# Sliding-window attention scores of the prompt tiles as two fp32r products of stacked high and low halves

## The reference, cut to what matters

```python
def swa_prompt(q, k, v, sinks_hg):          # CHUNK = 64, WINDOW = 128
    ...
    s = jnp.einsum('bcqhgd,bckhd->bchgqk', qc, kb) * SWA_SCALE
    key_chunk = jnp.arange(nc)[:, None] - WINDOW_CHUNKS + (jnp.arange(nk) // CHUNK)[None, :]
    s = jnp.where((key_chunk >= 0)[None, :, None, None, None, :], s, -jnp.inf)
    p = sink_softmax(s, sinks_hg)
    o = jnp.einsum('bchgqk,bckhd->bcqhgd', p, vb)
```

## Time and profile before

| | |
|---|---|
| median of 3 runs | 3121.53 us (3118.25 to 3123.85) |
| profiled execution, its own time | 3124.52 us |
| its span | 3122.7 us |
| PE busy in the span | 2974.5 us (95%) |
| DVE, ACT, POOL busy | 1613.0, 1026.0, 820.9 us |
| `phase_swa`, 1719 to 1925 us: PE busy | 195.88 of 206 us |
| the same: DVE, ACT busy | 91.87, 92.61 us |

### The profile page before, as it was taken

One profiled execution on the slowest core, in us unless ns is written; L12 is line 12 of the kernel. 1 busy time (PEld: TensorE's weight loads), 2 busy tenths in 40 slices (PEclk: granted clock), 3 DMA queues, 4 the chain that ended last, 5 costly groups with the idle time before them and its releaser, 6 DMA issues. The chain is left out here.

```text
span 3122.7 us, 42383 instructions
## 1 busy us (share of the span) xinstructions
PE 2974.5 (95%) x15759; PEld 2611.1 (84%) x15759; DVE 1613.0 (52%) x2600; ACT 1026.0 (33%) x2019; POOL 820.9 (26%) x703
## 2 busy tenths in 40 slices
PE   8899889998999999999998998998999999999997
PEld 7455468886889999999997898997889999999996
DVE  3566224556545555555556443445445555555556
ACT  5344122333332323222224453334342232322233
POOL 1245111111232333222326000112132233322235
PEclk9999899998999999999999998999999999999999
DMA  3100340103111111111112111113111111111112
GB/s 125 33 8 9 130 140 18 42 31 120 35 59 41 40 40 47 47 41 40 40 34 80 43 35 40 34 36 123 34 59 41 40 40 40 47 46 41 40 34 80
DMA packets 71943, 160.47 MB, mean 51 GB/s; under 512 B 19258, under 2 KB 33739, under 8 KB 70772
## 3 DMA queue, kind: packets, MB, share of 16 engines
q1 hardware_dynamic: 70676, 150.51, 15.1%
q0 software_dynamic: 1152, 8.39, 0.7%
HBM read 144.42 MB, written 15.11 MB: 51 GB/s over the span
## 5 line engine op out<-in xcount | busy, mean ns | idle before, releaser
L128 PE MATMUL psum<-xT_hi,tk_whi 128*128 128x384 f32 x2112 | 712.6, 337 | 7.5 <-ACT tk_u L2215 3.3
L129 PE MATMUL psum<-xT_lo,tk_whi 128*128 128x384 f32 x2112 | 711.2, 337 | 0.0
L130 PE MATMUL psum<-xT_hi,tk_wlo 128*128 128x384 f32 x2112 | 711.1, 337 | 0.0
L2413 DVE TENSOR_TENSOR x_or_mix<-x_or_mix,psum 128x512 f32<-128x512 f32 x684 | 466.0, 688 | 243.1 <-PE psum L130 242.8
L128 PEld LDWEIGHTS psum<-xT_hi,tk_whi 128*128 128x128 f32 x2112 | 398.4, 189 | 11.5 <-ACT tk_u L2218 6.1
L129 PEld LDWEIGHTS psum<-xT_lo,tk_whi 128*128 128x128 f32 x2112 | 398.3, 189 | 1.6
L130 PEld LDWEIGHTS psum<-xT_hi,tk_wlo 128*128 128x128 f32 x2112 | 398.2, 189 | 0.0
L2376 DVE SCALAR_TENSOR_TENSOR tk_c<-tk_u,tk_cw,tk_c 128x1168 f32<-128x1168 f32 x84 | 157.8, 1879 | 447.2 <-ACT tk_c L2226 447.2
L128 PE MATMUL psum<-tk_dhi,tk_gh 128*128 128x512 f32 x756 | 294.7, 390 | 1.7 <-ACT tk_u L2218 1.7
L130 PE MATMUL psum<-tk_dhi,tk_gl 128*128 128x512 f32 x756 | 295.0, 390 | 0.0
L129 PE MATMUL psum<-tk_dlo,tk_gh 128*128 128x512 f32 x756 | 294.9, 390 | 0.0
(11 more groups left out here) (378 smaller groups left out, 5310.8 us busy)
## 6 DMA issues: line engine op xcount, KB each, us to landing
tk_wraw<-in_w_up SPq DMA_DIRECT2D x88, 512.0 KB, 3.6
tk_draw<-in_w_down SPq DMA_DIRECT2D x44, 512.0 KB, 3.6
s_ckv<-in_c_ckv POOLq DMA_DIRECT2D x8, 1024.0 KB, 5.0
retw_raw<-in_w_ret SPq DMA_DIRECT2D x32, 256.0 KB, 3.4
tk_mix_wraw<-in_w_out SPq DMA_DIRECT2D x16, 512.0 KB, 4.0
glaw_raw<-in_w_gla SPq DMA_DIRECT2D x32, 192.0 KB, 3.1
x_or_mix<-in_xT SPq DMA_DIRECT2D x9, 512.0 KB, 9.4
tk_xin<-in_x_in SPq DMA_DIRECT2D x9, 512.0 KB, 3.5
```

The costliest lines, as they stand in the source:

```text
L128: nc.tensor.matmul(out, a[0], b[0], start=first, stop=False)
L129: nc.tensor.matmul(out, a[0], b[1], start=False, stop=False)
L130: return nc.tensor.matmul(out, a[1], b[0], start=False, stop=last)
L2413: nc.vector.tensor_tensor(x, x, PS[:, down_bank(n), :], ALU.add).then_inc(ad, 1)
```

## The change

The scores of the prompt tiles are computed in fp32r from rounded high parts and remainders. For each head there are two products over 128 rows: [qh; qh] by [kh; kl], and [ql; mask rows] by [kh; mask rows]. The product ql by kl is left out; it is below the precision kept. The buffers Q1, Q2, K1, K2 lie in the left half of `x_or_mix`, which is free in this phase. The sample tile keeps its fp32 product.

```diff
+    XMR = c.rounded("swa_halves", "x_or_mix", [P, NT, D])
+    K1, K2 = XMR[:, 0:TP, 0:P], XMR[:, 0:TP, P:2 * P]
+    Q1, Q2 = (XMR[:, 4 * x:4 * x + 4, 2 * P:4 * P].rearrange("p (s a) (b n) -> p s a b n", s=2, n=P) for x in range(2))
+    tiles_to = lambda n: n - n // NT
 # SP, after the weights and six small loads, ahead of w_a2b and the caches
+            sp.wait_ge(on, 2)
+            sp.dma_start(Pb[HD:HD + 8, 0, :], A["swa_q_rows"][:, 0:1024]).then_inc(rwl, 16)
+            sp.dma_start(Pb[HD:HD + 8, 1, :], A["swa_k_rows"][:, 0:1024]).then_inc(rwl, 16)
 # POOL, ahead of make_lo(0)
+            pool.wait_ge(on, 1)
+            nc.gpsimd.memset(Pb[:], 0.0).then_inc(on, 1)
 # PE, transposes(n): after pe.wait_ge(qkT, n)
+                    if n >= 2:
+                        pe.wait_ge(qkl, tiles_to(n - 1))
 # PE, scores(m), prompt tiles
-                        keys = KT[0:HD + 4, max(t - 1, 0) * P:(t + 1) * P]
-                        last = nc.tensor.matmul(o[:, 0:P] if t == 0 else o, QT[0:HD + 4, slot(t), h, :], keys, ...)
+                    pe.wait_ge(qkl, tiles_to(of_tile(i, t)))
+                    pe.wait_ge(rwr, 1)
+                        nc.tensor.matmul(o, Q1[:, *q], K1[:, near], start=True, stop=False, skip_group_check=True)
+                        last = nc.tensor.matmul(o, Q2[:, *q], K2[:, near], start=False, stop=True, skip_group_check=True)
 # PE, sums(1)
+                    pe.wait_ge(qkl, 2 * TP)
 # ACT, keep_qkT(n), prompt tiles
-                        nc.scalar.activation(QT[0:HD, slot(t), odd::2, :], src..., ACT.Copy)
+                        for copy in range(2):
+                            nc.scalar.activation(Q1[64 * copy:64 * copy + 64, slot(t), :, odd, :], src..., ACT.Copy)
-                nc.scalar.activation(KT[0:HD, t * P:(t + 1) * P], PS[0:64, 2, 2 * P:3 * P], ACT.Copy).then_inc(qkT, 1)
+                    nc.scalar.activation(K2[0:HD, t, :], src, ACT.Copy)
+                    nc.scalar.activation(K1[0:HD, t, :], src, ACT.Copy).then_inc(qkT, 1)
 # ACT, at the start of slot 1
+            def round_rows():
+                act.wait_ge(rwl, 32)
+                for s in range(2):
+                    nc.scalar.activation(Q2[HD:P, s]..., Pb[HD:P, 0, 512 * s:512 * s + 512]..., ACT.Copy)
+                nc.scalar.activation(K2[HD:P], Pb[HD:P, 1, :]..., ACT.Copy).then_inc(rwr, 1)
 # DVE, after step() of slot s, for s = 2 to 18 where tile s-1 is a prompt tile
+            def halves_lo(n):
+                dve.wait_ge(qkT, n + 1)
+                for odd in range(2):
+                    own = slice(64 * odd, 64 * odd + 64)
+                    nc.vector.tensor_tensor(Q2[0:HD, slot(t), :, odd, :], PS[own, 2, 0:2 * P]..., Q1[own, ...].bitcast(F), ALU.subtract)
+                nc.vector.tensor_tensor(K1[HD:P, t, :], PS[0:64, 2, 2 * P:3 * P], K1[0:HD, t, :].bitcast(F), ALU.subtract).then_inc(qkl, 1)
```

More of the change, by code:

```diff
@@ L69, in __init__, with rounded @@
         self.nc, self.A = nc, A
+        self.places = {}
     def sb(self, name, shape, dt=F):
-        return self.nc.alloc_sbuf_tensor(name, shape, dt)
+        t = self.nc.alloc_sbuf_tensor(name, shape, dt)
+        self.places[name] = self.nc.sbuf_base - 4 * int(np.prod(shape[1:]))
+        return t
+    def rounded(self, name, of, shape):
+        return self.nc.alloc_sbuf_tensor_at(name, shape, R, offset=self.places[of])
     def sem(self, name):
@@ L1291, in phase_swa @@
     (lg, lgk, ln, gt, su, suk, dsu, ach) = (c.sem("gate_" + s) for s in names)
+    qkl, rwl, rwr = (c.sem("swa_" + s) for s in ("qkT_lo", "rows_loaded", "rows_rounded"))
+    XMR = c.rounded("swa_halves", "x_or_mix", [P, NT, D])
+    K1, K2 = XMR[:, 0:TP, 0:P], XMR[:, 0:TP, P:2 * P]
+    Q1, Q2 = (XMR[:, 4 * x:4 * x + 4, 2 * P:4 * P].rearrange("p (s a) (b n) -> p s a b n", s=2, n=P) for x in range(2))
     SCALE = HD ** -0.5
@@ L1434, in scores @@
                 else:
+                    pe.wait_ge(qkl, tiles_to(of_tile(i, t)))
+                    pe.wait_ge(rwr, 1)
+                    near = slice(max(t - 1, 0), t + 1)
                     for h in range(4):
-                        o = PS[:, 4 + h // 2, (h % 2) * 256:(h % 2) * 256 + 256]
-                        keys = KT[0:HD + 4, max(t - 1, 0) * P:(t + 1) * P]
-                        last = nc.tensor.matmul(o[:, 0:P] if t == 0 else o, QT[0:HD + 4, slot(t), h, :], keys, start=True, stop=True,
-                                                skip_group_check=True)
+                        o = PS[:, 4 + h // 2, (h % 2) * 256:(h % 2) * 256 + (P if t == 0 else 256)].rearrange("p (t n) -> p t n", n=P)
+                        q = (slot(t), h // 2, h % 2)
+                        nc.tensor.matmul(o, Q1[:, *q], K1[:, near], start=True, stop=False, skip_group_check=True)
+                        last = nc.tensor.matmul(o, Q2[:, *q], K2[:, near], start=False, stop=True, skip_group_check=True)
                 last.then_inc(sc, 1)
@@ L1571, in keep_qkT @@
                     else:
-                        nc.scalar.activation(QT[0:HD, slot(t), odd::2, :], src.rearrange("p (q n) -> p q n", q=2), ACT.Copy)
+                        for copy in range(2):
+                            nc.scalar.activation(Q1[64 * copy:64 * copy + 64, slot(t), :, odd, :], src.rearrange("p (q n) -> p q n", q=2), ACT.Copy)
                 if i == 0:
                     nc.scalar.activation(gaT[0:16, t * P:(t + 1) * P], PS[0:16, 2, 3 * P:4 * P], ACT.Copy)
-                nc.scalar.activation(KT[0:HD, t * P:(t + 1) * P], PS[0:64, 2, 2 * P:3 * P], ACT.Copy).then_inc(qkT, 1)
+                src = PS[0:64, 2, 2 * P:3 * P]
+                if t == TP:
+                    nc.scalar.activation(KT[0:HD, t * P:(t + 1) * P], src, ACT.Copy).then_inc(qkT, 1)
+                else:
+                    nc.scalar.activation(K2[0:HD, t, :], src, ACT.Copy)
[3 more added lines that the diff above has]
+                for s in range(2):
+                    nc.scalar.activation(Q2[HD:P, s].rearrange("p a b n -> p a (b n)"), Pb[HD:P, 0, 512 * s:512 * s + 512].rearrange("p (a n) -> p a n", a=2), ACT.Copy)
+                nc.scalar.activation(K2[HD:P], Pb[HD:P, 1, :].rearrange("p (t n) -> p t n", n=P), ACT.Copy).then_inc(rwr, 1)
             def step(m):
@@ L1612, in _ @@
                 steps = STEPS.get(s, ())
+                if s == 1:
+                    round_rows()
                 if len(steps) == 2:
@@ L1662, in rotate @@
                 nc.vector.tensor_tensor(dst[:, :, 0:16], ta[:], tb[:], ALU.add).then_inc(qkr, 1)
+            def halves_lo(n):
+                i, t = where(n)
+                dve.wait_ge(qkT, n + 1)
+                for odd in range(2):
+                    own = slice(64 * odd, 64 * odd + 64)
+                    nc.vector.tensor_tensor(Q2[0:HD, slot(t), :, odd, :], PS[own, 2, 0:2 * P].rearrange("p (q n) -> p q n", q=2),
+                                            Q1[own, slot(t), :, odd, :].bitcast(F), ALU.subtract)
+                nc.vector.tensor_tensor(K1[HD:P, t, :], PS[0:64, 2, 2 * P:3 * P], K1[0:HD, t, :].bitcast(F), ALU.subtract).then_inc(qkl, 1)
             def take(m):
@@ L1733, in _ @@
                     step(steps[-1], s - 3 if 3 <= s < 3 + NT else None)
+                if 2 <= s <= TILES and where(s - 1)[1] != TP:
+                    halves_lo(s - 1)
                 if s == 15:
```

## The result

| | before | after |
|---|---|---|
| median | 3119.32 us (3115.53 to 3124.98, 20 runs) | 3124.83 us (3121.35 to 3129.3, 20 runs) |
| profiled execution, its own time | 3124.52 us | 3124.10 us |
| its span | 3122.7 us | 3122.2 us |

The ratio is 1.0017, with a 95% interval of 1.001 to 1.0023. The changed kernel is 5.5 us slower, where I had forecast 0.3 less. The time lies in the range of 3116 to 3127, but the direction is missed.

What follows compares the result with a forecast made beforehand. PE was taken as the bound, with ACT taking its place after the change; +2.8 up to slot 17, -2.4 and -0.8 in the tail and +0.1 at the start gave -0.3 us, median 3121.2 us, range 3116 to 3127.

Steps and rivals of the forecast that it cites:

- +2.8 up to slot 17: Slots 2 to 17: delays from ACT's copies and slot 8's wait outweigh the shorter scores, +2.8 us.
- -3.2 in the tail: Slots 18 and 19: shorter scores lie on the chain, -2.4 us at the lower clock and -0.8 us.
- What bounds the kernel: Whole phase: PE is the bound, busy 95% of the span; ACT is ready 1.3 us before PE asks.
- Scores on PE: Prompt-tile scores: 0.12 us per fp32r product instead of 0.23, saving PE 0.85 us in each of 14 units, 12 us.
- fp32r is no cheaper: Rival for the scores on PE: each product still takes 0.23 us, giving +3.2, 3124.4 us; chance 0.08.
- Copies on ACT: keep_qkT on ACT: three more copies per prompt tile put 1.05 us ahead of the copy for the values.
- What is late next: Values in slots 2 to 17 wait for ACT's later copy: changes per slot from -0.85 to +0.85 us.
- Cover: the projection of 4.2 to 4.4 us: DVE's halves_lo after write_out: hidden by the projection; in slot 18 uncovered, sums(1) held 0.6 us, but PE later anyway.
- the clock rival: PE's new pauses in slots 3, 4, 12 to 17 lower the clock: 3123 to 3126 (chance 0.09) or 3132 (0.08).
- the rival with one to three falls: One to three clock falls in slots 3, 4, 12 to 17, 1.4 us lost each: 3123 to 3126 us; chance 0.09.
- the sign that I had named against my forecast: Changed profile: a granted clock below 1 between 1810 and 1889 would make the prediction wrong.
- the tail's -2.4: Slot 18: shorter scores at the lower clock shorten the chain by 2.2 us; slot 17's +0.25 taken off again, -2.4.

Runs made afterwards that it cites:

- e13: The changed kernel with unread PE products filling its pauses everywhere, remainders left behind the write-out: 3118.42 us, ratio 0.9997 to the kernel before.
- e14: The changed kernel with unread PE products filling its pauses and the remainders of slots 17 and 18 ahead of the write-out: 3114.39 us, ratio 0.9979.
- e8: The changed kernel with DVE's remainders of slots 17 and 18 moved ahead of the write-out, no fills: 3123.13 us, ratio 1.0014 to the kernel before.
- e0: The changed kernel run again, unaltered, beside the kernel before: 3126.36 us, ratio 1.0012.
- e12: The changed kernel run once more, unaltered, in the last set: 3127.40 us, ratio 1.002 to the kernel before.
- e1: The changed kernel with five unread fp32r products ahead of the values in slots 3 to 7, 9 and 12 to 17: 3122.67 us, ratio 1.0009.
- e15: The kernel before with unread PE products in its pauses of slots 8, 18 and 20: 3114.22 us, ratio 0.9979 to the kernel before.
- e7: The changed kernel with ACT's copy for the values ahead of its projection copies and, in slot 8, take ahead of make_lo: 3107.78 us, ratio 0.9955.
- e3: The kernel before with only ACT's three added copies per prompt tile, scores still fp32, no remainders: 3119.76 us, ratio 0.9996.

## Why the prediction was wrong, point by point

**Where the 5.5 come from.** The forecast was +2.8 up to slot 17, -3.2 in the tail and +0.1 at the start. In after's trace against before's it was +7.6 up to the values of slot 17 and -6.7 from there to the next phase, so +1.0 for the phase. The larger part is not in these two traces: before's profiled execution stood 5.2 above the median of its 20 runs, after's 0.7 below its own. Half of before's executions took 3115.5 to 3118.3, and after has none under 3121.3.

**What bounds the kernel: right.** PE was the bound, and the lead of ACT over PE was what mattered.

**Scores on PE: right.** 0.12 from start to start (1769.95, 1770.07 in after's slot 5), as estimated, with a new stationary operand each time. The rule of the Trainium skill that speaks against it ("TensorE: Matmul & The Clock Gate", Part 3, "What overlaps and what doesn't") is contradicted by these rows: all rows of the array are used and the loads stay hidden. The rival "fp32r is no cheaper" fell with it.

**Copies on ACT: right in mechanism, a little too dear**: 0.94 instead of 1.05. The two copies of keys overlap as L1575 and L1581 did (0.17 apart), where I had taken 0.28.

**What is late next: right, except for the clock.** Changes of the single slots in after's trace, against forecast: slots 5 to 7 and 9 -0.22 (-0.20), slot 10 -0.77 (-0.85), slot 2 +0.68 (+0.74), slot 3 +0.67 (+0.76), slot 12 +0.94 (+0.85), slot 13 +0.44 (+0.46), slots 14, 16, 17 +0.22 (+0.25), slot 8 +0.94 (+0.85). Without falls the slots up to 17 give about +3.0, and I had +2.8. In after's trace, though, the values of slot 17 stand 7.6 later, counted from the phase's first product: 4.6 of it are falls, in slot 3 (1.5), slot 9 (1.5) and the longer one behind slot 8's pause (6.8 us at the lower level instead of 3.4, +1.6).

**The first step that failed: "Cover: the projection of 4.2 to 4.4 us. In slot 18 it has no such cover and can hold `sums(1)` up by 0.6, but at the lower clock PE is later anyway."** I saw that the last remainders have no cover, named only one of the two waits on `qkl` there, and put it at nothing. The transposes of slot 18 come ahead of `sums(1)`, and they wait for the remainders of slot 17. These stand behind a write-out that waits for PE. PE stands still for 1.67 us, and for 0.75 more ahead of the sums. With the other pauses filled this costs 5.0 +- 1.9 with what follows from it (e13 against e14; 3.9 in the traces). In the kernel as it was measured its price stays open: there the removal of the wait gave no gain that the runs can tell from zero (e8), since the clock falls behind it in any case. So this wait was missed, but it is not shown to be the 5.5.

**The second: the chance of the clock rival.** I gave falls in slots 3, 4 and 12 to 17 a chance of 0.09 (one to three, 3123 to 3126) and 0.08 (more), and let 1.4 us stand for each. They came, two in each of the traces of after, e0, e8 and e12, in slots 3, 5, 6, 9 and 13, so not only in the slots that I had named, and each cost 1.5. The median of 3124.8 lies where the rival with one to three falls had it, and the sign that I had named against my forecast, a granted clock below 1 between 1810 and 1889, is there (0.98). My 1.4 came from a window that ended at 1807.0; before's fall in slot 8 runs from 1804.1 to 1807.5, 3.4 us and not 2.9. The reason that I gave against the falls, that before has none between 1740 and 1800, holds only for a PE without pauses, as I said myself. What filling these pauses alone gives back is 2.4 +- 1.7 (e1). All falls together cost after 7.2 and before 5.9, a difference of 1.3 with an uncertainty of 2.6. The Trainium skill has a passage that I should have weighed ("TensorE: Matmul & The Clock Gate", Part 1, "A second HAM failure mode: psum-queue depth-cycling"): short idle times between groups of products can be enough to make the clock swing. The traces of after and e1 agree with it: a clock of 0.97 and 0.98 in the two groups with the pauses, 1.00 with them filled.

**The third: the tail's -2.4 was measured from one execution.** The profile of before was of an execution of 3124.5, with the clock down in slots 18 and 20. The median of before lies between such executions and those without. I took the difference inside that one trace, -3.2 with slot 19, and set it against the median. Where the tail runs at the higher clock up to slot 19, as in e15, that gain is not there: from the values of slot 17 to the next phase before takes 27.1 (e15), and after with the same kind of fills 28.5 with the wait of slot 18 (e13) and 24.4 without it (e14). In the trace on which the forecast was built this part took 35.4.

**The sum without the clock was near, in part by luck**: without falls and without the missed wait, after stands -0.4 +- 1.3 from before (e14 against e15), and -0.3 was forecast. But in the traces of the two, all up to the transposes of slot 17 adds +1.5 (slot 8 gives -0.2 under the fills, not +0.85), and what follows takes 2.4 away, at a clock that I had not assumed. The fills also shorten both tails.

**The better version** keeps the change and moves three things: the copy for the values ahead of the projection copies on ACT, `take` ahead of `make_lo` in slot 8, the remainders ahead of the write-out in slots 17 and 18. It runs at 3106.44 us (with a few unread products in slots 18 and 20), 0.9956 of before. The first two moves alone gave 0.9955 (e7); what the third adds there is not shown.

## What to carry to other kernels

When an added wait is "covered by the next projection", go through every place where the loop waits on that semaphore, the last turns above all, where the covering work is missing, and read what stands ahead of the releasing instruction in its engine's list. Shortening the bound engine's work by 12 us is worth nothing as long as another engine's list holds up the next step; moving one copy in that list turned a ratio of 1.0012 into 0.9978. And if single executions of a kernel differ by several us, take a step's price from the place in the trace, but not the total from one profile.

## What the hardware showed that I had not expected

- With pauses of 0.5 to 1.2 us ahead of the values in most slots, the granted clock fell to the lower level twice in each of four traces, besides slot 8 and the tail, at places that change between executions (1754.3 in one, 1773.3 in another, 1784.1 and 1852.4 in a third). With pauses in five slots only it did not fall there (e3, one trace). 0.6 us of unread products in each pause kept it at 1.00 (e1, e13, e14).
- Unread products on the bound engine made the old kernel 5.9 +- 1.5 us faster (e15).
- The two copies of keys on ACT start 0.17 apart, while the copy of the gate rows holds up the next one by 0.28, from the same bank and of the same duration. Why, no run here tells.
